# Key pages in four buffers: other ring places for cached rows, later output weights, another order of the first heads

## The reference: what is computed

```
q_lat, q_rope, ckv, krope = project(rmsnorm(x))          # 8 heads, latent 256, rope 64
prompt:  s = (q_lat . ckv + q_rope . krope) * scale, causal; o = softmax(s) @ ckv
sample:  past = cache[page_table]                        # 8 sequences x 8 pages x 128 rows
         s = [q . past keys, q . new keys] * scale;      o = softmax(s) @ [past rows, new rows]
out = (o @ w_uv) @ w_o
```

## Time and profile before

| | |
|---|---|
| median of 3 runs | 1193.99 us (1192.52 to 1194.03) |
| profiled execution, its time | 1194.44 us |
| its span | 1192.7 us |
| TensorE busy | 1065.9 us (89%) |
| weight loads busy | 656.7 us (55%) |
| VectorE, ScalarE, GpSimd busy | 369.3, 189.9, 115.0 us |
| mean granted clock of TensorE | 0.961 |
| moved by DMA | 306.02 MB, mean 257 GB/s |

### The profile page before, as it was taken

How to read it: one execution, slowest core, us unless ns; L and a number is a source line. 1 busy time by engine, 2 the same in 40 slices (tenths; PEclk the granted TensorE clock), 3 DMA queues, 4 the chain that set the end, 5 groups by cost and what they waited for, 6 DMA issues and landing times.

```text
span 1192.7 us, 14363 instructions
## 1 busy us (share of the span) xinstructions
PE 1065.9 (89%) x5248; PEld 656.7 (55%) x5248; DVE 369.3 (31%) x929; ACT 189.9 (16%) x389; POOL 115.0 (10%) x152
## 2 busy tenths in 40 slices
PE   6978699999988886999999999999999998787693
PEld 5747366544433332777777777777644443332272
DVE  4545214322221101562227444221422221110164
ACT  2122112211111101231112110001211111011121
POOL 1333000111111111000000000000111111110101
PEclk9989799899999999999999999999979999999897
DMA  9758282499999996933333323333269999999501
GB/s 367 301 166 257 74 359 108 150 397 421 417 420 419 419 420 256 421 144 138 115 132 141 106 106 106 106 132 138 98 245 411 419 418 418 419 420 382 223 33 40
DMA packets 62613, 306.02 MB, mean 257 GB/s; under 512 B 13746, under 2 KB 23186, under 8 KB 30546
## 3 DMA queue, kind: packets, MB, share of 16 engines
q1 hardware_dynamic: 45936, 275.73, 58.3%
q0 software_dynamic: 13632, 22.58, 5.7%
q10 hardware_dynamic: 2978, 6.80, 1.5%
HBM read 308.10 MB, written 21.08 MB: 276 GB/s over the span
## 4 chain that ended last, share of the span: by engine, by line
PE 64%; DMA 23%; issue 5%; DVE 3%; SPq 3%; ACT 1%; POOL 0%; POOLq 0%; DVEq 0%; ACTq 0%
DMA ring_sb<-stream 23%; PE ps L1607 16%; PE ps L1462 10%; PE ps L1655 8%; PE ps L1471 4%; PE ps L1540 3%; PE ps L1377 3%; PE ps L1160 2%; PE ps L1420 2%; PE ps L1151 2%; PE ps L1202 1%; SPq L292 1%; SPq L293 1%; PE ps L1558 1%; PE ps L1556 1%
## 5 line engine op out<-in xcount | busy, mean ns | idle before, releaser
L1462 PE MATMUL ps<-ring_sb,scr_sb 128*64 128x512 f32 x1024 | 236.4, 609 | 41.0 <-DMA ring_sb<-stream 41.0
L1607 PE MATMUL ps<-hn_sb,ring_sb 128*128 128x288 f32 x768 | 194.9, 408 | 0.0
L1462 PEld LDWEIGHTS ps<-ring_sb,scr_sb 128*64 128x64 f32 x1024 | 78.7, 140 | 194.6 <-issue 194.5
L1607 PEld LDWEIGHTS ps<-hn_sb,ring_sb 128*128 128x128 f32 x768 | 142.6, 190 | 37.3 <-DVE hn_sb L700 0.3
L1471 PE MATMUL ps<-ring_sb,scr_sb 128*64 128x512 f32 x512 | 121.4, 617 | 2.1 <-ACT scr_sb L598 1.9
L986 DVE SCALAR_TENSOR_TENSOR scr_sb<-ps,scr_sb 128x256 f32<-128x256 f32 x32 | 15.5, 483 | 267.0 <-ACT scr_sb L594 267.0
L1655 PE MATMUL ps<-scr_sb,ring_sb 128*128 128x288 f32 x384 | 95.3, 407 | 0.0
L1655 PEld LDWEIGHTS ps<-scr_sb,ring_sb 128*128 128x128 f32 x384 | 72.2, 190 | 19.4
L1471 PEld LDWEIGHTS ps<-ring_sb,scr_sb 128*64 128x64 f32 x512 | 34.9, 141 | 61.7 <-issue 57.4
L1540 PE MATMUL ps<-scr_sb,ring_sb 128*128 128x288 f32 x256 | 64.3, 406 | 0.0
L352 POOL DMA_INDIRECT scr_sb<-hn_rows,scr_sb x32 | 32.4, 1014 | 301.5 <-DVE scr_sb L963 276.7
(11 more groups left out here) (258 smaller groups left out, 1098.6 us busy)
## 6 DMA issues: line engine op xcount, KB each, us to landing
ring_sb<-stream SPq DMA_DIRECT2D x249, 1024.0 KB, 18.3
scr_sb<-key_pages SPq DMA_DIRECT2D x64, 192.0 KB, 3.4
ring_sb<-row_pages POOLq DMA_DIRECT2D x64, 128.0 KB, 3.5
scr_sb<-y_rows POOLq DMA_DIRECT2D x8, 512.0 KB, 5.0
hn_rows<-scr_sb ACTq DMA_DIRECT2D x4, 512.0 KB, 3.1
h_sb<-x SPq DMA_DIRECT2D x1, 1152.0 KB, 5.6
scr_sb<-bs ACTq DMA_DIRECT2D x1, 640.0 KB, 12.9
scr_sb<-p ACTq DMA_DIRECT2D x2, 288.0 KB, 5.2
```

The source lines that it names most:

```text
L1462: last = mm(ps[64 * a:64 * a + 64, 2 + b, :], xT[:, k, 64 * a:64 * a + 64], slot(a + 2 * (k // 4))[:, (k % 4) * 512:(k % 4) * 512 + 512], ...
L1607: last = mm(bank((i + 1) % 4, T), ring(s, (i % 2) * D + k * P, P), hn_t[:, k, :], start=(k == 0), stop=(k == KD - 1))
```

## The change

It has five parts.

- Key chunks go into four buffers, chunk n into buffer n % 4. The two new ones, `keys_r`, lie in ring places 0 to 2. Chunks 2 and 3 wait for `slot_free` 2 and 3, chunk n from 4 on for `key_free` n - 3. SyncE issues all eight chunks in a row after slot 6.
- The cached rows go to ring places 7 to 11 and 3 to 5. The first five chunks wait for no slot, only for `x_sum` (a VectorE sum early in the projections); the last three for `slot_free` 4, 5 and 6, which the first query-latent tile now gives instead of `scores(0)`.
- Slots 7 to 11 (S_UV and S_O) are loaded after the key chunks, each when one more row chunk has been used. Slots 12 to 14 wait for all key chunks, slots from 15 on for all row chunks.
- Head 0 stands before the sample chunks 0 and 1, and head 1 before chunks 2 and 3. VectorE normalises head 0 and takes the maxima of head 1 before the sample query copies.
- Three semaphores are merged: `ptab_in` into `par_in`, `s_ot_ps` into `s_o_ps`, and `ql_ps` counts once a head in place of once a tile.

```diff
--- before.py
+++ after.py
@@ -42,7 +42,8 @@
 NEG = -1e30
 
 SLOT, RING = 2048, 12
-ROW_POS = [0, 1, 2, 3, 4, 5, 6, 11]
+ROW_POS = [7, 8, 9, 10, 11, 3, 4, 5]
+ROW_AFTER = [0, 0, 0, 0, 0, 4, 5, 6]
 S_IN, S_QB, S_UK, S_UV, S_O = 0, 3, 6, 7, 8
 S_PROJ = [12, 149]
 S_MOE = [13, 150]
@@ -142,6 +143,8 @@
     ola_s = A.take(KV)
     snew = A.take(NS_)
     keys = A.take(2 * 4 * 2 * 384).rearrange("p (u b g n) -> p u b g n", u=2, b=4, g=2)
+    keys_r = ring_t[:, 0:3 * SLOT].rearrange("p (u b g n) -> p u b g n", u=2, b=4, g=2)
+    key_buf = [keys[:, 0], keys[:, 1], keys_r[:, 0], keys_r[:, 1]]
     rt = pt_s.rearrange("p g r -> p (g r)")[:, 0:2 * T].rearrange("p (a t) -> p a t", a=2)
     sm = A.take(32)
     rn = pt_s.rearrange("p g r -> p (g r)")[:, 2 * T:3 * T]
@@ -283,30 +286,32 @@
 
         def load_keys(chunk):
 
-            u = chunk % 2
-            if chunk >= 2:
-                sp.wait_ge(sem("key_free"), chunk - 1)
+            u = chunk % 4
+            if chunk in (2, 3):
+                sp.wait_ge(sem("slot_free"), chunk)
+            if chunk >= 4:
+                sp.wait_ge(sem("key_free"), chunk - 3)
             for b in range(4):
                 for pg in range(2):
                     at = (chunk // 4 * 4 + b) * PAGES + 2 * (chunk % 4) + pg
                     page = sp.value_load(ptab[0:1, at:at + 1], min_val=0, max_val=io["n_phys"] - 1)
-                    sp.dma_start(keys[:, u, b, pg, :],
+                    sp.dma_start(key_buf[u][:, b, pg, :],
                                  io["key_pages"][bass.ds(page, 1)].rearrange("a p n -> (a p) n")
                                  ).then_inc(sem(f"key_full{u}"), 16)
 
         sp.dma_start(h_t[:, :, :], io["x"]).then_inc(sem("x_in"), 16)
         for s in range(S_UK + 1):
             load_slot(s)
-        sp.wait_ge(sem("ptab_in"), 16)
-        load_keys(0)
-        load_keys(1)
-        for s in range(S_UV, RING - 1):
+        sp.wait_ge(sem("par_in"), 32)
+        for chunk in range(8):
+            load_keys(chunk)
+        for s in range(S_UV, RING):
+            sp.wait_ge(sem("rows_free"), s - S_UV + 1)
             load_slot(s)
-        for chunk in range(2, 8):
-            load_keys(chunk)
-
-        sp.wait_ge(sem("rows_free"), 8)
-        for s in range(RING - 1, 2 * RING):
+        sp.wait_ge(sem("key_free"), 8)
+        for s in range(RING, 2 * RING):
+            if s == RING + ROW_POS[5]:
+                sp.wait_ge(sem("rows_free"), 8)
             load_slot(s)
         def load_rounds(r0, r1):
 
@@ -433,10 +438,11 @@
                                    ).then_inc(sem(f"y12_in{t}"), 16)
 
 
-        pool.wait_ge(sem("ptab_in"), 16)
+        pool.wait_ge(sem("par_in"), 32)
+        pool.wait_ge(sem("x_sum"), 1)
         for c in range(8):
-            if c < 7:
-                pool.wait_ge(sem("slot_free"), c + 1)
+            if ROW_AFTER[c]:
+                pool.wait_ge(sem("slot_free"), ROW_AFTER[c])
             for b in range(4):
                 for pg in range(2):
                     at = (4 * (c // 4) + b) * PAGES + 2 * (c % 4) + pg
@@ -478,7 +484,7 @@
 
 
         act.dma_start(par[:, :], io["par"]).then_inc(sem("par_in"), 16)
-        act.dma_start(ptab[:, :], io["ptab"]).then_inc(sem("ptab_in"), 16)
+        act.dma_start(ptab[:, :], io["ptab"]).then_inc(sem("par_in"), 16)
         act.dma_start(const[:, :], io["const"]).then_inc(sem("const_in"), 16)
         act.dma_start(aconst, io["aconst"]).then_inc(sem("aconst_in"), 16)
 
@@ -508,7 +514,7 @@
         act.dma_start(w_r[:, :, :, :], io["w_r"]).then_inc(sem("wr_in"), 16)
         act.dma_start(b_r[:, :, :], io["b_r"]).then_inc(sem("wr_in"), 16)
         for h in range(H):
-            act.wait_ge(sem("ql_ps"), 2 * h + 1)
+            act.wait_ge(sem("ql_ps"), h + 1)
             nc.scalar.activation(ql[:, h, 0, :], bank(QL_BANK[2 * h % 4], T), ACT.Copy).then_inc(sem("ql_a"), 1)
 
         def exp_prompt(h):
@@ -718,7 +724,7 @@
 
         nc.vector.memset(eps[:, 0:1], 1e-6).then_inc(sem("eps"), 1)
         nc.vector.memset(eps[:, 1:2], 1e-5).then_inc(sem("eps"), 1)
-        dve.wait_ge(sem("par_in"), 16)
+        dve.wait_ge(sem("par_in"), 32)
         dve.wait_ge(sem("x_in"), 16)
         for k in range(KD):
             nc.vector.tensor_scalar(hn_t[:, k, :], h_t[:, k, :], par[:, G_MIX[0] + k:G_MIX[0] + k + 1], None, ALU.mult
@@ -790,7 +796,7 @@
 
         def take_ql(h0, h1):
             for h in range(h0, h1):
-                dve.wait_ge(sem("ql_ps"), 2 * h + 2)
+                dve.wait_ge(sem("ql_ps"), h + 1)
                 nc.vector.tensor_copy(ql[:, h, 1, :], bank(QL_BANK[(2 * h + 1) % 4], T)).then_inc(sem("ql_d"), 1)
 
         def max_prompt(h):
@@ -833,11 +839,11 @@
             nc.vector.tensor_copy(pt_s[0:NS_, 8, :], ps[0:NS_, 6, 0:P]).then_inc(sem("s_pt"), 1)
 
         def take_ola(r):
-            dve.wait_ge(sem("s_o_ps"), r + 1)
+            dve.wait_ge(sem("s_o_ps"), 2 * r + 1)
             nc.vector.tensor_copy(ola_s, bank(7, KV)).then_inc(sem("s_ola"), 1)
 
         def take_ol(r):
-            dve.wait_ge(sem("s_ot_ps"), r + 1)
+            dve.wait_ge(sem("s_o_ps"), 2 * r + 2)
             for c in range(2):
                 nc.vector.tensor_copy(
                     ql[:, :, c, NP_ + 16 * r:NP_ + 16 * r + 16].rearrange("p h (b s) -> p b h s", b=4),
@@ -847,6 +853,8 @@
         take_ql(0, 6)
         max_prompt(0)
         take_ql(6, H)
+        norm_prompt(0)
+        max_prompt(1)
         dve.wait_ge(sem("ql_a"), H)
         dve.wait_ge(sem("ql_d"), H)
         for c in range(2):
@@ -858,8 +866,6 @@
                     qs[32 * a:32 * a + 32, 2].rearrange("p b (h e s) -> p b h e s", h=H // 2, e=2)[:, :, :, e, :],
                     qr[64 * a + 32 * e:64 * a + 32 * e + 32, :, NP_:T].rearrange("p h (b s) -> p b h s", b=DEC_B)
                 ).then_inc(sem("qs"), 1)
-        norm_prompt(0)
-        max_prompt(1)
         for h in range(H):
             if h == 3:
                 norm_sample(0)
@@ -1227,7 +1233,9 @@
                     if h >= 2:
                         pe.wait_ge(sem("ql_a" if c == 0 else "ql_d"), h - 1)
                     last = mm(bank(QL_BANK[(2 * h + c) % 4], T), ring(S_UK, h * KV + c * P, P), qn[:, h, :], start=True, stop=True)
-                    last.then_inc(sem("ql_ps"), 1)
+                    if c == 0:
+                        free_with(last)
+                last.then_inc(sem("ql_ps"), 1)
 
         def scores(h):
             u = h % 2
@@ -1261,15 +1269,14 @@
             return qs[0:RO, 2, 4 * r + b, :] if c == 2 else qs[:, c, 4 * r + b, :]
 
         def s_chunk(r, cc):
-            u = cc % 2
-            pe.wait_ge(sem(f"key_full{u}"), 128 * (2 * r + cc // 2 + 1))
+            pe.wait_ge(sem(f"key_full{cc}"), 128 * (r + 1))
             if cc == 0 and r == 1:
                 pe.wait_ge(sem("s_pt"), 3)
             if cc == 0 and r == 0:
                 pe.wait_ge(sem("qs"), 6)
             for c in range(3):
                 for b in range(4):
-                    mov = keys[:, u, b, :, c * P:(c + 1) * P] if c < 2 else keys[0:RO, u, b, :, 256:384]
+                    mov = key_buf[cc][:, b, :, c * P:(c + 1) * P] if c < 2 else key_buf[cc][0:RO, b, :, 256:384]
                     last = mm(ps[32 * b:32 * b + 32, 4 + cc // 2, (cc % 2) * 256:(cc % 2) * 256 + 256],
                               q_of(r, b, c), mov, start=(c == 0), stop=(c == 2))
             last.then_inc(sem("key_free"), 1)
@@ -1309,7 +1316,7 @@
             pe.wait_ge(sem("s_ola"), r + 1)
             for c in range(2):
                 last = nc.tensor.transpose(ps[:, 6, P + c * P:2 * P + c * P], ola_s[:, c * P:(c + 1) * P], ident)
-            last.then_inc(sem("s_ot_ps"), 1)
+            last.then_inc(sem("s_o_ps"), 1)
 
         def head(h, between=()):
             turn_p(h)
@@ -1328,9 +1335,8 @@
         scores(1)
         ql_tiles(6, H)
         owe(1)
-        s_chunk(0, 0), s_chunk(0, 1)
-        head(0), s_chunk(0, 2)
-        head(1), s_chunk(0, 3)
+        head(0), s_chunk(0, 0), s_chunk(0, 1)
+        head(1), s_chunk(0, 2), s_chunk(0, 3)
         head(2)
         head(3), s_turn(0)
         head(4), s_chunk(1, 0), s_chunk(1, 1)
```

## The result

The changed kernel took 1178.95 us, median of 4 runs (1176.49 to 1181.83), the kernel before 1193.26 us beside it (1192.42 to 1194.03). The ratio is 0.9882, 95% interval 0.986 to 0.9904: 1.2% faster. The profiled execution was the slowest of the four, 1181.8 us with a span of 1180.1.

The account below looks back on a forecast made before the run. SyncE's key-page issuing was taken as the bound: four buffers save 19.2 us, head 0 first loses 4.3, other parts cost nothing. The gain of 15.0 us from 1194.0 gives 1179.0, range 1175 to 1184.

Parts of the forecast that it names:

- The bound: Key stage of the sample products: ends at first buffer release plus 48 SyncE page issues in a row plus a landing.
- Four buffers, 19.2 us: Key loads: 32 pages, not 48, behind the first release save 18.0 us; a SyncE pause and slower steps add 1.2.
- First head leads, 4.3 us lost: Head 0 before the sample chunks: first page behind the release goes at 79.6 instead of 75.3.
- Gain 15.0 us: Last key page lands at 117.0 instead of 132.0, and everything behind it comes 15 us earlier.
- The waits left, 2 and 7 us: TensorE, early in the sample products, still waits for keys: about 2 us before chunk 6, 7 before chunk 7.
- Weights late at no cost: Slots 7 to 11, loaded as value products release them, arrive before they are needed; costed at nothing.
- the cover: UV weights at L1352: needed 15.8 us after their release, a lone slot lands in 4.6, so 11 us to spare.
- Row pages at no cost: GpSimd's earlier row pages run beside the first weights, which still land before they are needed; costed at nothing.
- half-share case: Row pages take half the bandwidth from 10 us on: last of the first seven weight slots lands at 40, not 25.1.
- The clock at the same price: Around chunk 7, one low-clock stretch instead of two costs the same as before, with up to 1.5 us to be had.
- The whole wait goes: Rival, chance 0.04: pages issued in 0.8 us or less end the key wait and low clock; 29 us gain, 1165.
- The clock falling in the early gaps: Smaller-gain rival, chance 0.13: gaps before and in head 0 lower the clock, first release 4.2 us later; 1183, up to 1188.

Follow-up runs that it names:

- e2: Changed kernel with two key buffers instead of four, all else of the change kept: 1198.98 us, ratio 1.0055 to the kernel before.
- e6: Changed kernel with SyncE reading the 32 page numbers of chunks 4 to 7 into registers before the first key release: 1167.09 us, ratio 0.9791.
- e1: Changed kernel with TensorE's and VectorE's order of before (sample chunks 0 and 1 ahead of head 0), four buffers kept: 1173.66 us, ratio 0.9851.
- e11: The changed kernel itself, unedited, run once more beside other kernels on one chip: 1179.08 us, ratio 0.9877 to the kernel before.
- e4: Changed kernel with weight slots 7 to 11 all waiting until all eight row chunks are used: 1185.29 us, ratio 0.9926 to the kernel before.
- e5: Changed kernel with row pages started after the first slot release instead of after the sum of squares: 1177.85 us, ratio 0.9862.
- e8: Kernel before, two key buffers kept, with only the page numbers of chunks 2 to 7 read ahead into registers: 1181.29 us, ratio 0.99.
- e7: Changed kernel with page numbers of chunks 4 to 7 read ahead and the order of before (sample chunks first): 1165.2 us, ratio 0.976.
- e3: Changed kernel with unread products (two and six of 128 x 512) on TensorE before the waits for chunks 6 and 7: 1175.68 us, ratio 0.9874.

## Why the prediction was right

**The bound.** That SyncE's page issues are the path and TensorE is early was right. e2 and e6 show it from both sides: 16 more pages behind the release cost 20 us, 18 of them in issues, and half the time per page takes both waits away. One reading was too simple. In the kernel before, the 48 pages do not all hang on the first release: chunk 6 waited for TensorE's release by chunk 4 at 111.81, and the chain runs over TensorE from 96.17 to there. The two paths were within 0.9 us of each other, so the sum hardly notices.

**Four buffers, 19.2 us.** Measured 20.1 in the trace (138.38 - 118.25), 20.0 in the medians and 20.6 by the ratios.

**First head leads, 4.3 us lost.** e1 gives 4.5 in the trace. Worked forward, head 0 was to start at 73.1 (73.37), its apply step at 75.95 (76.20), the first chunk at 77.2 (77.71 in the timeline), the first page of chunk 4 to go at 79.6 (80.45).

**Gain 15.0 us.** The trace gives 13.8 at the last chunk and 13.4 at L1358, the medians 14.3. The 1.2 us between 15.0 and 13.8 are three small terms: 0.3 of the whole timeline, already there at the first query tile (38.17 against 37.89 in the earlier trace rows), about 0.6 more up to the first page, and 31 x 0.015 = 0.5 in the mean step (1.140 for 1.125), which is the long issue at 97.19, less 0.15 in the landing (2.41 for 2.56). In part this is one execution and not the kernel: in e11, the same program, the first page goes at 79.67, the last at 114.91 and chunk 7 starts at 117.41, 14.6 us before the kernel before. From there to L1358 the changed kernel takes 22.5 us and the kernel before 22.1, which is the step from 13.8 to 13.4. The median came out at 1178.95 where 1179.0 was forecast. That closeness is luck: the gain was 0.7 us smaller than forecast, the kernel before came out 0.7 us lower beside it (1193.26 for 1194.0), and single runs lie 5 us apart.

**The waits left, 2 and 7 us.** 2.52 and 6.07. Chunk 6 ran at the lower clock (2.58 in place of 1.64), which takes its difference out of the second wait.

**Weights late at no cost.** Right, and e4 measures the cover at 11.2 us against 11 worked out. A wait here costs more than its length, since L1358 then runs slower.

**Row pages at no cost.** Right (e5). The first slots are 3 us later, far from the half-share case that was allowed for. The two queues did share the engines. In 13 to 28 us the DMA engines were busy all the time, and the 13 row pages issued there landed after 5.4 to 6.5 us, while the seven key pages of SyncE issued there took 9.2 to 18.7. So a row page doesn't wait for all that SyncE has asked for before it. This is the taking of turns that the Trainium skill states ("DMA: Bandwidth & Descriptors", "Queues, rings and completion order"), and the trace agrees with it. What failed to come was the half share: GpSimd asks for one page of 128 KB every 1.14 us, 115 GB/s, and its transfers took 20% of the engines' time in that stretch. Two queues that both always have work are not shown here.

**The clock at the same price.** Right within half a microsecond: one stretch at the lower level (granted 0.50 from 112 to 126 us), from the wait for chunk 7 to the value products behind it, and 22.5 us from chunk 7 to L1358 where before took 22.1.

**The rivals.** "The whole wait goes" was priced at 1165 us for pages issued in 0.8 us or less. It did not happen in this change, and e6 then made it happen, at 1167. The clock falling in the early gaps did happen, in one profiled execution, for 1 us or so and not for 4.2.

What stays open is whether e6 gives anything back behind L1358, and why the clock in the second expert layer differs between executions of one program; no run tried to steer it. The merged semaphores were not tried alone; VectorE's first wait is now put down to the page table, with 5.6 us as in e8, which has the semaphores of before, and the first query tile starts 0.3 us later than before.

## What to carry to other kernels

When an engine waits for many small transfers, look at the issuing queue first: the time between two issues, times the number that stands behind the release, set when the last chunk came here (35.4 us of issues against 2.4 of landing). A queue that computes addresses can do so before it waits for the buffer, which costs registers and no memory. More buffers and an earlier release are the other two ways. More buffers, with the ring places they need, add to the read-ahead (16 us between e8 and e7), since the landing that stands behind each release with two buffers is hidden with four. An earlier release adds to more buffers (e1), but only one microsecond of the trace on top of both (e7), because TensorE is the path by then. Ask of each part of a change whether it moves the release that the path hangs on: one part of this one did so by 4 us in the wrong direction, hidden behind a gain of 20.

## What the runs showed of the hardware

A key page costs SyncE 1.10 to 1.14 us with its register load and 0.515 to 0.6 us when the page number is already in a register. Pages issued 1.14 us apart land 2.5 us after their issue (median, 79 to 117 us of the changed kernel), those 0.5 to 0.6 us apart 5.2 us (e6, 78 to 98 us):

```profile
DMA to landing us min/median/max: 2.3/2.5/3.7
```

```profile
DMA to landing us min/median/max: 2.6/5.2/6.2
```

A gap of 2.35 us in TensorE's work lowered its clock in one profiled execution (e4, granted 0.57 in 74 to 76 us) and left it at 1.00 in six others with a gap of 2.3 to 2.4 us (the changed kernel, e2, e3, e5, e6, e11). A wait of 3.5 us before L1358 made that product 1.7 us longer (9.69 against 8.00, granted clock 0.66 in 145 to 150 us of e4). Beside a queue of SyncE that kept the DMA engines busy, GpSimd's pages of 128 KB landed 5.4 to 6.5 us after their issue, and SyncE's of 192 KB after 9.2 to 18.7 (issued in 13 to 28 us of the changed kernel).
